# An attention stage regrouped: doubled prompt tiles, sample row b beside head pair b, V pages first in each slot

## The reference, cut to what matters

```python
def fox_attend(q, cq, qpos, k, ck, kpos, v):
    s = einsum('bqhd,bkhd->bhqk', q, k) * scale + cq - ck      # cumulative log forget values
    s = where(kpos <= qpos, s, -inf)
    return einsum('bhqk,bkhd->bqhd', softmax(s), v)

def fox_sample(...):                # 8 sequences, 4 queries each
    kp, vp = cache_k[page_table], cache_v[page_table]          # 32 pages of 128 rows x 16 heads x 64
    ...
y = (o * silu(z)) @ w_out_attn ; x = x + y ; rms_norm(x)
```

## Time and profile before

| | us |
|---|---|
| median of three runs | 2247.55 |
| profiled execution, its own time | 2248.77 |
| span of the profiled execution | 2247.0 |
| first block, up to the first scores of pair 0 | 1397.15 |
| rounds 0 to 7 | 704.98 |
| output projection and end | 144.87 |

### The profile page before, as it was taken

One profiled execution on the slowest core, in us unless ns is written; L12 is line 12 of the kernel. 1 busy time (PEld: TensorE's weight loads), 2 busy tenths in 40 slices (PEclk: granted clock), 3 DMA queues, 4 the chain that ended last, 5 costly groups with the idle time before them and its releaser, 6 DMA issues. The chain is left out here.

```text
span 2247.0 us, 39897 instructions
## 1 busy us (share of the span) xinstructions
PE 1930.5 (86%) x15120; PEld 1416.0 (63%) x15120; DVE 1129.9 (50%) x1810; ACT 563.5 (25%) x1253; POOL 349.8 (16%) x401
## 2 busy tenths in 40 slices
PE   4999999999999788999999996877877768768798
PEld 3876877777787566877877774544444434344475
DVE  4444534544563687677677763333334333333423
ACT  4211121121121421111111111333433334233431
POOL 0000000000000034544445442011011010110010
PEclk9999999999999898999999997568889788687899
DMA  4111111111111479999999997247678676685761
GB/s 136 38 44 48 43 40 56 35 49 47 39 49 38 161 232 308 343 312 341 348 325 330 317 323 253 105 154 248 218 212 258 224 233 225 203 257 181 276 243 71
DMA packets 218393, 413.65 MB, mean 184 GB/s; under 512 B 18593, under 2 KB 129858, under 8 KB 218014
## 3 DMA queue, kind: packets, MB, share of 16 engines
q1 hardware_dynamic: 148764, 222.15, 30.6%
q0 software_dynamic: 51648, 180.71, 23.5%
q10 hardware_dynamic: 17874, 9.27, 1.4%
HBM read 370.85 MB, written 41.94 MB: 184 GB/s over the span
## 5 line engine op out<-in xcount | busy, mean ns | idle before, releaser
L1180 DVE STREAM_TRANSPOSE kt<-k_raw 128x1024 f32<-128x1024 f32 x256 | 310.8, 1234 | 145.7 <-DMA k_raw<-in_cache_k_dram,k_idx 120.0
L347 POOL DMA_INDIRECT k_raw<-in_cache_k_dram,k_idx x256 | 259.4, 1013 | 444.4 <-DVE kt L1180 284.6
L765 PE MATMUL ps_a<-h_hi,w_hi 128*128 128x512 f32 x656 | 265.7, 405 | 1.7 <-DVE w_lo L1017 1.7
L766 PE MATMUL ps_a<-h_lo,w_hi 128*128 128x512 f32 x656 | 258.7, 394 | 0.0
L767 PE MATMUL ps_a<-h_hi,w_lo 128*128 128x512 f32 x656 | 258.6, 394 | 0.0
L1693 DVE TENSOR_REDUCE pp_nm<-ps_a 128x1 f32<-128x128 f32 (+3 forms) x64 | 48.5, 758 | 306.4 <-PE ps_a L1421 306.4
L1017 DVE TENSOR_TENSOR w_lo<-w_raw,w_hi 128x1024 fp32r<-128x1024 f32 x97 | 109.1, 1124 | 171.3 <-ACT w_hi L594 169.0
L1443 PE MATMUL b<-con,p_p 128*128 128x128 f32 x432 | 98.4, 347 | 102.7 <-DVE p_p L1701 48.4
L765 PE MATMUL ps_b<-h_hi,w_hi 128*128 128x512 f32 x384 | 157.2, 409 | 0.0
L766 PE MATMUL ps_b<-h_lo,w_hi 128*128 128x512 f32 x384 | 152.1, 396 | 0.0
L767 PE MATMUL ps_b<-h_hi,w_lo 128*128 128x512 f32 x384 | 152.0, 396 | 0.0
(11 more groups left out here) (291 smaller groups left out, 3131.8 us busy)
## 6 DMA issues: line engine op xcount, KB each, us to landing
v_pg<-in_cache_v_dram SPq DMA_DIRECT2D x256, 512.0 KB, 5.1
w_raw<-in_w_in_pool_dram SPq DMA_DIRECT2D x32, 512.0 KB
w_raw<-in_w_in_attn_dram SPq DMA_DIRECT2D x32, 512.0 KB
w_raw<-in_w_out_pool_dram SPq DMA_DIRECT2D x16, 512.0 KB
s_scr<-ss_st ACTq DMA_DIRECT2D x64, 128.0 KB
s_in<-s_scr POOLq DMA_DIRECT2D x16, 512.0 KB, 5.0
d_sb<-decay POOLq DMA_DIRECT2D x32, 256.0 KB, 6.9
z_scr<-x_st SPq DMA_DIRECT2D x8, 528.0 KB, 4.6
```

What stands on the lines that cost most here:

```text
L347: pool.indirect_dma_start(k_raw[:, k, :], None, cache_rows, bass.IndirectOffsetOnAxis(ap=k_idx[:, u, k:k + 1], axis=0)).then_inc(k_full[k] ...
L765: nc.tensor.matmul(ps, ah, bh, start=j == 0, stop=False)
L766: nc.tensor.matmul(ps, ah, bl, start=False, stop=False)
L1180: V.transpose(kt[u % 2][:, :, 32 * k:32 * k + 32], k_raw[:, k, :].rearrange("p (i c) -> p i c", c=32)).then_inc(dve_kt, 1)
```

## The change

Both blocks become one, without the meeting point, and the loops over pairs are written out, as are the projection groups 6 and 7. In group 7 the last z tile's first unit of sample scores moves behind the second half of the tile.

- qa, ka and v_pr exist twice. The loads for pair b + 1 are issued by GpSimd when pair b - 1 has finished its scores and values; those of pair 0 by SyncE at projection tile (7, 2), and those of pair 1 by GpSimd after the last unit.
- Sequence b's exponentials, turns and pages run in round b (before: b + 1). Its scores, new scores and maximum are made during round b - 1, those of sequence 0 ahead of round 0. The first score halves and z_t are loaded by SyncE.
- A slot on TensorE is now: prompt_values of s - 1, four V pages, the turns of head 0 and head 1, in slots 1, 3 and 5 sample_turn, then scores of s + 1. In slot 0 the pages stand behind the turns. Scores of the next pair's slot 0 stand in slot 7, and prompt_values of slot 7 in the next pair's slot 0.
- The transposes use three banks, x (b6), y (in ps_b) and z (b7), where they used two.
- w_out rows 4 to 7 are loaded ahead of the last sequence's pages 8 and on, rows 0 to 3 after its page 15; rows 4 to 7 are split in round 7, where z_hi and z_lo of blocks 0 and 1 are also made. The output projection starts with rows 4 to 7 and holds no sample pages or turns. x1_t, xs_c and fn_b lie at other addresses.

```diff
+        at_qk = (AT_F, AT_K + 8192)
+        qa = [place(f"qa{i}", [AUG, 2, SEQ], F32, big_at(at_qk[i])) for i in range(2)]
+        ka = [place(f"ka{i}", [AUG, 2, SEQ], F32, big_at(at_qk[i] + 2048)) for i in range(2)]
+        v_pr = [place(f"v_pr{i}", [P, TT, P], F32, big_at((AT_F + 4096, 15168)[i])) for i in range(2)]
+        w_at = [big_at(AT_F + 1024 * k if k < 4 else 11072 + 1024 * (k - 4)) for k in range(KT8)]
...
+        def score_half(eng, b, half):
+            c = slice(512 * half, 512 * half + 512)
+            landed = ld_d[half] if b else ld_d_first[half]
+            eng.dma_start(s_in[:, :, c], s_scr[b, :, :, c]).then_inc(landed, 16)
+            for hh in range(2):
+                src = decay[b, hh].rearrange("c g u k -> (c g) (u k)")[:, c]
+                eng.dma_start(d_sb[:, hh, c], src.unsqueeze(1).to_broadcast([32, NQ, 512])).then_inc(landed, 16)
...
@@ sync_project, end of the projection @@
+                    if (f, n) == (7, 2):
+                        sp.wait_ge(st_dec, 16 * 16)
+                        sp.wait_ge(st_lf, 64)
+                        sp.wait_ge(st_q, 32)
+                        sp.wait_ge(st_k, 32)
+                        sp.wait_ge(st_vtm, 16)
+                        qk_pair(sp, 0)
+                        v_pair(sp, 0)
             store_k(KT8 - 1)
             store_k_rows(KT8 - 1)
+            store_v_rows(KT8 - 1)
+            sp.wait_ge(tile_done, CR_W + C_L0 + 1 + 4 * KT8)
+            for i in range(2):
+                sp.wait_ge(st_s[i], 16 * QUADS // 2)
+            score_half(sp, 0, 0)
+            score_half(sp, 0, 1)
...
@@ waits for the last stores @@
+            sp.dma_start(z_t[:, 0, :], z_scr[0]).then_inc(ld_z[0], 16)
+            sp.dma_start(z_t[:, 1:KT8, :], z_scr[1:KT8].rearrange("f p t -> p f t")).then_inc(ld_z[1], 16)
...
             sp.wait_ge(pe_qk, UNITS)
             for p in range(VR):
                 v_load(sp, 1, p).then_inc(v_full[p], 16)
-                store_v_rows(KT8 - 1)
...
@@ gpsimd_project: the same loads leave @@
-                    if u == 60:
-                        ...
-                        qk_pair(pool, 0)
-                        v_pair(pool, 0)
...
@@ banks of the transposes @@
+        def fills(s, h):
+            n = QBLOCKS[s] + 1
+            if n <= 4:
+                return [(0, n, "xz"[h])]
+            if h == 0:
+                return [(0, 4, "x"), (4, n - 4, "z")]
+            return [(0, 3, "y"), (3, min(4, n - 3), "x")] + ([(7, 1, "z")] if n == 8 else [])
+        def t2_bank(key):
+            return {"x": b6[:, :], "y": ps_b[:, 512 + P:1024], "z": b7[:, :]}[t2_name(key)]
...
@@ sync_attend @@
+            for k in range(4, KT8):
+                w_out_rows(k)
             for p in range(VR, PAGES):
                 v_page(NB, p)
+                if p == 15:
+                    sp.wait_ge(pe_s, 16 * (NB - 1))
+                    for k in range(4):
+                        w_out_rows(k)
...
@@ gpsimd_attend @@
+            for b in range(NB):
+                if b < NB - 1:
+                    pool.wait_ge(dve_s, b * N_S + 4)
+                    score_half(pool, b + 1, 1)
+                if 0 < b < NB - 1:
+                    pool.wait_ge(pe_s, 16 * b)
+                    qk_pair(pool, b + 1)
+                    pool.wait_ge(pe_pvp, SLOTS * b)
+                    v_pair(pool, b + 1)
+                if b > 0:
+                    sample_out(b - 1)
+                if b < NB - 2:
+                    pool.wait_ge(dve_s, (b + 1) * N_S + 2)
+                    score_half(pool, b + 2, 0)
...
@@ tensor_attend; sample_values is now sample_pages and sample_last @@
+            def pair(b):
+                for s in range(SLOTS):
+                    if s:
+                        prompt_values(b, s - 1)
+                    elif b:
+                        prompt_values(b - 1, SLOTS - 1)
+                    if s == 0:
+                        sample_turn(b, 0)
+                    if s == 7 and b < NB - 1:
+                        new_scores(b + 1)
+                    if s:
+                        sample_pages(b, s, range(4))
+                    prompt_turn(b, s, 0)
+                    prompt_turn(b, s, 1)
+                    if s == 0:
+                        sample_pages(b, s, range(4))
+                    if s == SLOTS - 1:
+                        sample_last(b)
+                    if s in (1, 3, 5):
+                        sample_turn(b, (s + 1) // 2)
+                    if s < SLOTS - 1:
+                        scores(b, s + 1)
+                    elif b < NB - 1:
+                        scores(b + 1, 0)
+                    if s == 5:
+                        new_turn(b)
...
@@ scalar_attend @@
+            def pair(b):
+                for s in range(SLOTS):
+                    prompt_exp(b, s, 0)
+                    prompt_exp(b, s, 1)
+                    if s == 0:
+                        sample_evac(b, 0)
+                    prompt_evac(b, s, 0)
+                    if s in (1, 3, 5):
+                        sample_exp(b, (s + 1) // 2)
+                    prompt_evac(b, s, 1)
+                    if s in (1, 3, 5):
+                        sample_evac(b, (s + 1) // 2)
+                    if s == 5:
+                        new_evac(b)
+                    if s == 7 and b < NB - 1:
+                        sample_exp(b + 1, 0)
+                    if b == NB - 1 and s in (2, 3, 4, 5):
+                        act.wait_ge(dve_s, N_S * NB)
+                        high_w(s + 2)
+                    if b == NB - 1 and s in (4, 6):
+                        high_z(s // 2 - 2)
...
@@ vector_attend @@
+            def pair(b):
+                more = b < NB - 1
+                for s in range(SLOTS):
+                    prompt_max(b, s, 0)
+                    prompt_max(b, s, 1)
+                    if s:
+                        gate(b, s - 1)
+                    elif b:
+                        gate(b - 1, SLOTS - 1)
+                    if s == 7 and more:
+                        new_scores(b + 1)
+                    prompt_norm(b, s, 0)
+                    prompt_norm(b, s, 1)
+                    if s % 2 == 0 and more:
+                        sample_scores(b + 1, s // 2)
+                    if s == 4 and more:
+                        queries(b + 1)
+                    if s == 6:
+                        sum_exp(b)
+                    ...
+                if more:
+                    common_max(b + 1)
+                sample_out(b)
+            queries(0)
+            for o in range(4):
+                sample_scores(0, o)
+            new_scores(0)
+            common_max(0)
+            for b in range(NB):
+                pair(b)
```

More of the change, by code:

```diff
@@ new lines, in v_pair, with qk_pair @@
+        def v_pair(eng, b):
+            eng.dma_start(v_pr[b % 2][:, :, :], v_prompt[0, 0].rearrange("(t p) h d -> p t (h d)", p=P)
+                          [:, :, P * b:P * b + P]).then_inc(ld_v[b % 2] if b else ld_v_first, 16)
+        def qk_pair(eng, b):
+            for src, dst in ((q_aug, qa[b % 2]), (k_aug, ka[b % 2])):
+                eng.dma_start(dst[:, :, :], src[2 * b:2 * b + 2, :, :].rearrange("h d t -> d h t"))\
+                    .then_inc(ld_qk[b % 2] if b else ld_qk_first, 16)
@@ new lines, in mix_tile @@
+                    product = V.scalar_tensor_tensor(t1[:, c], ps[:, c], sc_t[:, 4 * g + d:4 * g + d + 1], t2[:, c],
+                                                     ALU.mult, ALU.mult)
+                    if half:
+                        product.then_inc(dve_mf, 1)
+                        dve.wait_ge(dve_mf, 4 * g + d + 2)
+                    else:
+                        link(product)
+                    link(V.tensor_copy(y_hi[:, d % 2, c], t1[:, c]))
+                    low = V.tensor_tensor(y_lo[:, d % 2, c], t1[:, c], y_hi[:, d % 2, c].bitcast(F32), ALU.subtract)
@@ new lines, in mix_tile, with out_piece @@
+                    if half:
+                        low.then_inc(dve_m, 1)
+                    else:
+                        dve.wait_ge(act_b7, 1 + B7 * g + B7_AT["m", d] + 1)
+                        V.tensor_tensor(y_s[:, d % 2, :], ym_s[:, :], sz_s[:, :], ALU.mult).then_inc(dve_m, 1)
+            def out_piece(g, n, j):
+                c = NCH * g + n
+                half = slice(512 * (j % 2), 512 * (j % 2) + 512)
+                dve.wait_ge(smp_used, c + 1 + CR_W)
+                V.tensor_tensor(x_s[:, half], x_s[:, half], b6[0:64, :], ALU.add).then_inc(dve_px, 1)
+                for u in range(TT):
+                    if u < TT - 1:
+                        dve.wait_ge(pe_o, (4 * g + j) * (TT - 1) + u + 1)
+                    else:
+                        dve.wait_ge(tile_done, c + 1 + CR_W)
+                    V.tensor_tensor(x_p[:, u, half], x_p[:, u, half], out_b[u % 2][:, :], ALU.add).then_inc(dve_o, 1)
@@ new lines, in log_forget_sums @@
+            def log_forget_sums():
```

(32 more changed lines are left out.)

2417 lines of the change are left out of this document (1140 added, 1277 removed).

## The result

| | before | after |
|---|---|---|
| median us (range, runs) | 2246.24 (2240.04 to 2249.08, 4) | 2063.06 (2057.64 to 2067.14, 4) |
| ratio, 95% interval | | 0.9186, 0.9157 to 0.9216 |
| span of the profiled execution | 2247.0 | 2062.9 |
| first block, up to round 0 | 1397.15 | 1379.34 |
| rounds 0 to 7 | 704.98 | 573.81 |

The forecast was 2051 and the range 2008 to 2125. The time is 12 us above the forecast.

What follows compares the result with a forecast made beforehand. The kernel before was taken as bound by TensorE's waits, chiefly for ka, and low clock, with DMA the next bound; 1404 + 8 x 67 + 110 = 2050 of span gave 2051 us, range 2008 to 2125.

Steps and rivals of the forecast that it cites:

- The doubled tiles: Start of each round: the 7.7 us wait for ka goes; 2.4 us of TensorE wait remain in slot 0.
- TensorE's path: Rounds: 56 us of matmul work plus 7 of waits in slots 0, 1, 3 and 5, 63 a round.
- DMA as the bound: Rounds: 64 us of DMA work at a share of 0.96 gives 66.7, taken as 67 a round; chance 0.60.
- the rival of late pages: Rounds: TensorE stops at the head of slots, the clock falls between, rounds of 75 to 78, 2128 us; chance 0.18.
- its signs: Rounds: expected 65 to 70 us each, with a DMA share of 0.9 or more and PEclk above 0.9.
- The two queues: Rounds: GpSimd's loads beside the pages take up to half the DMA rate, lengthening a round by at most some 11 us.
- The passage: Projection to round 0: first page at about 1405, round 0 in effect at 1404, range 1397 to 1415.
- The rival with 1.2 GHz throughout: Rounds: the clock stays low, 106 us a round, 2369 us, slower than before; chance 0.03.
- Two of the prediction's readings of the clock: Before kernel: slots 0 and 1 of each round run at 1.2 GHz; round 0 shows the clock can stay there throughout.
- The end: After the last values: 34.3 us leave the 144.87, so 110 stays, bounds 105 and 120.
- Sum: Whole kernel: 1404 + 8 x 67 + 110 = 2050 us of span; passage +7, rounds -169, end -35.

Runs made afterwards that it cites:

- pages_before_z: The changed kernel, but SyncE issues V pages 0 to 3 ahead of z_t's loads before round 0; 2057.09 us.
- half_pages: The changed kernel, but each V page load brings only its first 512 columns, with the same count of loads and matmuls; 2033.43 us.
- spread_loads: The changed kernel with GpSimd's loads for coming pairs spread over the round, same bytes, and sample_out moved ahead of them; 2042.17 us.
- two_blocks: The changed kernel with the meeting point of all engines put back between projection and attention; 2068.55 us.
- quarter_pages: The changed kernel, but each V page load brings only 256 of 1024 columns, TensorE's work unchanged; 2005.94 us.

## Why the prediction was right, and where its steps were off

- **The doubled tiles** (7.7 us a round go, 2.4 come back in slot 0). The wait for ka went, as forecast. In the old order they bring 34 us in all, and part of the gap comes back as a longer wait for s_sb. In the new order less came back than forecast: TensorE's waits for p_p came to only 0.6 us a round (4.2 over seven), 0.7 in slot 0 of round 3.
- **TensorE's path, 56 of work + 7 of waits = 63.** Measured without transfer limits: 55.3 + 4.1 = 59.4 in the best rounds, 60.4 on average. The work, 56.2 by its terms, was right to 0.9 us. The waits were oversized: slots 1, 3 and 5 cost (9.9 + 9.0) / 7 = 2.7 us a round in the change and not 4.6, slot 0 under 1 and not 2.4.
- **DMA as the bound, 64 / 0.96 = 66.7, taken as 67.** Rounds 1 to 7 took 475.2 us, 67.9 each, so the size was right within a microsecond. That transfers set it is shown: with a quarter of the page bytes rounds are 59.4 to 61.4. But the form was wrong. I had a steady stream that fills a round to 0.96. The share is 0.9 on average, 1.0 and more for 28 us and 0.80 in the 38 us behind them, and round 3 is TensorE's path of 59.4 plus 5.9 of idle time by late pages plus 3.6 of low clock, most of it after them. This is the mechanism of the rival of late pages, at a lower price than its 76. It comes near 67 because the path was 3.6 us shorter than I counted: on a path of 63 the same 9.5 us would have made a round of 72 or 73. That the two errors cancel is luck. And the same bytes, spread, save 20 us (rounds 1 to 6 are 65.7 on average, down to 62.0), so 66.7 was no floor. Of its signs, rounds 1 and 2 missed: round 1 took 70.71 us, with a share of 0.86 and a clock of 0.88, and round 2's clock was 0.90.
- **The two queues.** I gave the pages' slow landing beside GpSimd's loads as something that speaks against the change. It did: 7.8 us a page for 4.9, and 18.77 for the one in the chain. The rows of 1617 to 1637 us, by queue (packets, MB, share of the packet time of 16 engines), SyncE's pages first:

```profile
q1 hardware_dynamic: 1053, 3.82, 63.1%
q0 software_dynamic: 738, 1.76, 39.7%
```

  GpSimd's queue takes 39.7% of the time for 31% of the bytes, and the pages get 3.82 MB / 20 us = 191 GB/s where TensorE at full pace wants 282. The Trainium skill (DMA: Bandwidth & Descriptors, Queues, rings and completion order) says that a DMA engine turns from queue to queue by packets; the trace agrees in that neither queue is shut out, and shows the price that a byte count hides.
- **The passage, round 1 at 1404 + 67 = 1471.** It was 1477.95, 7 us late. The mis-sized term is the load of the transfers ahead of round 0. The first page was used at 1414.26 and not at 1405. Some of this is a slip in the sum: 27 us from 1382 on end at 1409. Some is the rate: from 1379.34 to 1405.43 the DMA share was 1.03 at 300 GB/s and not 337, and by it 9 MB last until 1412. SyncE's queue stood for 10.55 us over one store (L533), and the page issues came only at 1396.71. The score halves were late as well, landed at 1395.46 and not at 1392, so that prompt_max of slot 0 ran at 1404.09 and not by 1399. The first page alone is not what the 7 us hang on: in pages_before_z it is in time, and round 0 is as long. Nor are all 7 us a matter of round 0: over eight kernels here with the same first block, the change among them, the first scores ran between 1374.8 and 1382.7.
- **Clock.** The rival with 1.2 GHz throughout did not occur: the means of rounds 1 to 7 are 0.88 to 0.97, with 0.57 where pages are late (1630 to 1642). Two of the prediction's readings of the clock went too far. Slots 0 and 1 did not run at 1.2 GHz in each round before: in round 3 one head's eight-block scores, at 1667.83, already take 1.98 us. And the row of round 0, clock 0.52 at 68.8 busy us of 82, shows that the clock can stay low there, but no run here shows how busy TensorE would have had to be.
- **The end, 110.** Measured 109.75, with no idle time before the first product.
- **Sum.** +7 at round 1's start, +6 over seven rounds, 0 at the end: 2050 + 13 = 2063, the span.

What stays open is how the gain besides the tiles, 149 us, divides among the edits. By stages, the end is 35. The place of the pages alone is worth 45. In the rounds the trace says what went (102.2 us of short waits to 24.8, and 56.4 us of matmul time by the clock), but the third bank, the sample row beside its own pair, and the sample turns of odd slots were not tried apart.

## What to carry to other kernels

When a wait that recurs once a round is removed, ask what else used its pause: here the pages caught up in it, and the next bound appeared at the very same place of the round. Read the DMA share in steps of a few microseconds and not by the round, since a share of 0.9 can be 28 us of full engines and 40 with room. Count the short waits as well as the long one: before, they cost TensorE 102 us in seven rounds and the wait for ka 46. Before fewer bytes, try to issue the same bytes apart (20 us here), and then to put work that waits for a transfer in two places of a slot instead of all in one (13 us, at the edge of what could be told).

## What I had not expected of the hardware

- A DMA share of 0.65 over a round of half_pages still holds 23.2 us of waits for a transfer: from 1596 to 1612 the engines were full at 181 to 256 GB/s, and from 1620 to 1624 nearly empty (a share of 0.02).
- The rate at full engines goes with what they carry: 237 GB/s while GpSimd's queue takes 46.9% of the packet time beside the pages (1618 to 1630), 377 while it takes 14.0% (1630 to 1642).
- An issuing engine can be held by one DMA issue for long: 10.55 us for a store on SyncE's queue at 1385.06, behind the loads of z_t. The same store took 12.19 us in spread_loads, and 2.04 in pages_before_z, where it stands ahead of the large load of z_t. But in two_blocks, with the order of the change, it took 0.90, so the order alone does not decide it.
- The low clock is a second price of a late transfer: in round 3, 5.9 us more of idle time went with 3.6 us more of matmul time. Up to 1.7 us of this can also come in a round without a late page, as quarter_pages shows.
